# Seven block products in place of eight in the in-projections of two feed-forward stages

## The reference, cut to what matters

```python
def swiglu(x, w_in, w_out):                     # x (T, 1024), w_in (1024, 2*2816), w_out (2816, 1024)
    a, b = jnp.split(x @ w_in, 2, axis=-1)
    return (jax.nn.silu(a) * b) @ w_out

h = h + 0.5 * rms_norm_2(swiglu(rms_norm_2(h, g_ffn1_pre), w_ffn1_in, w_ffn1_out), g_ffn1_post)
...                                             # mixer
h = h + 0.5 * rms_norm_2(swiglu(rms_norm_2(h, g_ffn2_pre), w_ffn2_in, w_ffn2_out), g_ffn2_post)
```

## Time and profile before

| | us |
|---|---|
| three runs | 2240.53, 2245.5, 2245.35 |
| median | 2245.35 |
| the profiled execution, its own time | 2243.71 |
| its span in the trace | 2241.9 |
| PE busy in the span | 2103.8 (94%) |
| DVE busy | 993.0 (44%) |
| ACT busy | 725.9 (32%) |
| POOL busy | 624.9 (28%) |

### The profile page before, as it was taken

The page is one execution under the profiler, slowest core; times in us unless marked ns, Lnnn a source line. Parts: engine busy times, 40 slices in busy tenths (PEclk is TensorE's granted clock), DMA queues, the critical chain, the costliest instruction groups (busy, mean ns, idle before and its releaser), DMA issues.

```text
span 2241.9 us, 28339 instructions
## 1 busy us (share of the span) xinstructions
PE 2103.8 (94%) x11650; PEld 1754.6 (78%) x11650; DVE 993.0 (44%) x1483; ACT 725.9 (32%) x919; POOL 624.9 (28%) x152
## 2 busy tenths in 40 slices
PE   4999989999979999989999997999999979999997
PEld 3697777888757666589999996878788768888885
DVE  7374587656366666442222326232333252223224
ACT  6531345222245555332121123343232232221222
POOL 1331323344200000024433441221244314444440
PEclk6998999999979999989999997999999969999997
DMA  8122114554127999612222221211122212222220
GB/s 257 39 76 93 57 57 132 188 178 160 38 94 277 343 346 341 211 57 77 93 94 94 83 85 38 76 38 57 57 94 94 94 38 94 94 94 94 94 94 38
DMA packets 175177, 261.03 MB, mean 116 GB/s; under 512 B 12169, under 2 KB 140858, under 8 KB 175086
## 3 DMA queue, kind: packets, MB, share of 16 engines
q1 hardware_dynamic: 173550, 257.65, 34.5%
q10 hardware_dynamic: 1536, 2.10, 0.3%
HBM read 257.62 MB, written 2.11 MB: 116 GB/s over the span
## 4 chain that ended last, share of the span: by engine, by line
PE 89%; DVE 8%; ACT 2%; issue 1%; DMA 1%; DVEq 0%; SPq 0%; ACTq 0%
PE PS L704 68%; PE PS L1236 7%; PE PS L1258 4%; DVE Hf L2101 1%; PE PS L1390 1%; DVE macc L2167 1%; DVE Hf L2082 1%; PE PS L1202 1%; PE PS L764 1%; PE PS L1278 1%; DVE R L2113 1%; PE PS L1342 1%; PE PS L779 1%; PE PS L906 0%; PE PS L1160 0%
## 5 line engine op out<-in xcount | busy, mean ns | idle before, releaser
L663 POOL TENSOR_TENSOR w_lo<-w_raw,w_hi 128x2048 fp32r<-128x2048 f32 x133 | 620.3, 4664 | 1527.9 <-ACT w_hi L1509 1527.9
L704 PE MATMUL PS<-HH,w_hi 128*128 128x512 f32 (+1 forms) x1936 | 602.9, 349 | 31.8 <-DVE HL L2075 27.3
L704 PE MATMUL PS<-HL,w_hi 128*128 128x512 f32 (+1 forms) x1936 | 600.6, 348 | 0.0
L704 PE MATMUL PS<-HH,w_lo 128*128 128x512 f32 (+1 forms) x1936 | 597.6, 346 | 0.0
L1509 ACT ACTIVATE w_hi<-w_raw 128x2048 fp32r<-128x2048 f32 x133 | 254.8, 1915 | 713.5 <-DMA w_raw<-in_w_ffn_in 296.0
L704 PEld LDWEIGHTS PS<-HH,w_hi 128*128 128x128 f32 x1936 | 339.8, 191 | 84.4 <-issue 35.9
L704 PEld LDWEIGHTS PS<-HH,w_lo 128*128 128x128 f32 x1936 | 339.4, 191 | 45.8
L704 PEld LDWEIGHTS PS<-HL,w_hi 128*128 128x128 f32 x1936 | 339.3, 191 | 44.8
L2798 DVE TENSOR_TENSOR actf<-PS,sg 128x528 f32<-128x528 f32 (+1 forms) x44 | 30.8, 699 | 428.8 <-PE PS L704 428.8
L2809 DVE TENSOR_TENSOR yacc<-yacc,PS 128x528 f32<-128x528 f32 (+1 forms) x176 | 122.3, 695 | 106.2 <-PE PS L704 106.2
L2691 DVE TENSOR_TENSOR m_lo<-m_raw,m_hi 128x2048 fp32r<-128x2048 f32 x56 | 128.3, 2292 | 77.5 <-ACT m_hi L1842 76.8
(11 more groups left out here) (429 smaller groups left out, 2583.9 us busy)
## 6 DMA issues: line engine op xcount, KB each, us to landing
w_raw<-in_w_in SPq DMA_DIRECT2D x49, 1024.0 KB, 5.0
w_raw<-in_w_ffn_in SPq DMA_DIRECT2D x44, 1024.0 KB, 4.9
m_raw<-in_w_exp_gate SPq DMA_DIRECT2D x56, 512.0 KB, 4.2
m_raw<-in_w_exp_up SPq DMA_DIRECT2D x56, 512.0 KB, 5.3
m_raw<-in_w_exp_down SPq DMA_DIRECT2D x56, 512.0 KB, 4.8
w_raw<-in_w_ffn_out SPq DMA_DIRECT2D x22, 1024.0 KB, 4.8
mod_late<-in_w_mod SPq DMA_DIRECT2D x16, 1024.0 KB, 5.3
mod_early<-in_w_mod SPq DMA_DIRECT2D x8, 1024.0 KB, 11.8
```

The costliest lines, as they stand in the source:

```text
L663: pool.tensor_tensor(w_lo[:, s, :], w_raw[:, s, :], w_hi[:, s, :].bitcast(F32), ALU.subtract).then_inc(split, 1)
L704: ins = mm(o, l, r, **k)
```

## The change

The in-projection of a gate or up chunk is a product of a 2 by 2 block matrix of weights (two halves of the 1024 features by two halves of the 256 hidden ones) with a 2 by 2 block matrix of activations (the same two halves of the features by two halves of the tokens). Before, its eight block products are made one by one. After, there are seven (Strassen's method in the variant of Winograd): four sums of weight blocks, four of activation blocks, seven products, seven sums of products.

- Weights: DVE makes the four sums (`weight_sums`, each of 512 values a partition): one in place in `w_raw`, three in a new tile `wx_raw`. ACT and POOL split `wx_raw` as well (1536 values), after the chunk's 2048. ACT's high copy of `w_raw` and POOL's subtraction now wait for DVE's sums.
- Activations: `h_blocks` and `split_blocks` make and split the four sums once a stage, on DVE, ACT and POOL; each step handles four slices of T/2 columns, and PE waits for whole blocks.
- PE: 7 products of 12 matmuls of T/2 columns in place of 96 of 264 columns or 48 of 512. Two products share a PSUM slot; a chunk takes four slots, as many as there are.
- DVE: `block_sums` makes seven sums of 264 or 256 columns for each gate and up chunk, each with one operand in PSUM. ACT copies the first product to `fp` ahead of them. The silu is then computed by ACT in `sg` in place. DVE multiplies `actf` by `sg`, both now in SBUF and both tiles at once (1056 or 1024 values), ACT makes `ah`, DVE makes `al`.
- Order: DVE's `weight_sums` of the next gate chunk stands between the gate sums and the up sums of a unit, that of the next up chunk after the fourth down tile. Those of chunks 0 and 1 stand after tiles 4 and 6 of the step before the stage, that of chunk 2 before the clearing of `yacc`.

```diff
+            def h_blocks(n, T):
+                H, base = T // 2, HH_AT_FF[n]
+                pool.wait_ge(hh_ready, base + KT)
+                pool.tensor_tensor(HL[:, 4:8, 0:H], Hf[:, 4:8, 0:H], HH[:, 4:8, 0:H].bitcast(F32), ALU.subtract).then_inc(hp_ready, 1)
+                pool.tensor_tensor(HXr[:, 1, :, 0:H], Hf[:, 4:8, H:T], Hf[:, 0:4, H:T], ALU.subtract).then_inc(t3_ready, 1)
+                pool.wait_ge(hh_ready, base + KT + 3)
...
+            def split_seven(c, s, more=0):
+                pool.wait_ge(wx_ready, seven_made(c) + 1 + more * 2)
+                split_chunk(c, s, more)
+                pool.wait_ge(hix_done, seven_made(c) + 1 + more * 2)
+                pool.tensor_tensor(wx_lo[s][:, :, :, :], wx_raw[s][:, :, :, :], wx_hi[s][:, :, :, :].bitcast(F32),
+                                   ALU.subtract).then_inc(splitx, 1)
...
+            def seven_products(T, h_from=None):
...
+                for n in range(7):
+                    if n == 3:
+                        pe.wait_ge(splitx, xcount["n"] + 1 + xcount["more"])
...
+                    if n % 2 == 0:
+                        s = W.claim()
...
+                    for k in range(4):
+                        for x, (l, r) in enumerate(((0, 0), (0, 1), (1, 0))):
+                            ins = product(PS[:, s, n % 2, 0:H], left[l][n][:, k, :], right[r][n][:, k, :],
+                                          start=k == 0 and x == 0, stop=k == 3 and x == 2)
+                    if n % 2 == 1 or n == 6:
+                        W.made(ins)
...
             def next_hi():
...
+                if seven(c):
+                    act.wait_ge(wn_ready, seven_made(c) + 1 + rounds * 2)
+                else:
+                    act.wait_ge(w_in_sem[c % RING], 16 * (c // RING + 1) + rounds * 16)
...
+                if seven(c):
+                    act.wait_ge(wx_ready, seven_made(c) + 1 + rounds * 2)
+                    af(wx_hi[c % RING][:, :, :, :], wx_raw[c % RING][:, :, :, :], ACT.Copy).then_inc(hix_done, 1)
...
+                def unit(n, par):
+                    first_product()
                     next_hi()
+                    silu(n)
+                    first_product()
                     next_hi()
+                    product_hi(n, par)
...
+            def weight_sums(c):
...
+                dve.wait_ge(w_in_sem[s], 16 * (c // RING + 1) + more * 16)
+                a11, a12, a21, a22 = weight_blocks(w_raw[:, s, :])
+                x = wx_raw[s]
+                tt(x[:, 1], a11, a21, ALU.subtract)
+                tt(a21, a21, a22, ALU.add).then_inc(wn_ready, 1)
+                dve.wait_ge(wn_ready, n + more * 2)
+                L(tt(x[:, 0], a21, a11, ALU.subtract))
+                tt(x[:, 2], a12, x[:, 0], ALU.subtract).then_inc(wx_ready, 1)
...
                 W.release(stt(R[:, m, META:TALL], ps(s), modc[:, 40 + m:41 + m], R[:, m, META:TALL], ALU.mult, ALU.add))
+                if m in (4, 6):
+                    weight_sums(FF_AT[0] + m // 2 - 2)
...
+                def block_sums(dst):
+                    s0 = W.arrive()
...
+                    dve.wait_ge(fp_ready, n_["fp"] + n_["rounds"] * 2)
+                    tt(dst[:, 0, 0:H], fp[:, 0:H], PS[:, s0, 1, 0:H], ALU.add)
...
+                    s1 = W.arrive()
+                    u_ = L.mark(tt(fu[:, 0:H], fp[:, 0:H], PS[:, s1, 1, 0:H], ALU.add))
+                    L.wait(u_)
+                    w_ = L.mark(tt(dst[:, 0, H:T], fu[:, 0:H], PS[:, s1, 0, 0:H], ALU.add))
+                    dve.sem_inc(free[s0], 1)
...
+                def ups(n, par, more=0):
+                    block_sums(actf)
+                    dve.wait_ge(gate_silu, base + n + 1)
+                    tt(actf[:, :, 0:T], actf[:, :, 0:T], sg[:, :, 0:T], ALU.mult).then_inc(actf_ready, 1)
+                    dve.wait_ge(ah_ready, base + n + 1)
+                    tt(al[:, par, :, 0:T], actf[:, :, 0:T], ah[:, par, :, 0:T].bitcast(F32), ALU.subtract).then_inc(moe_act, 1)
...
+                def down(then=None):
                     for m in range(KT):
                         s = W.arrive()
                         y = sv(yacc[:, m, 0:T], T)
                         W.release(tt(y, y, ps(s, T), ALU.add))
+                        if m == 3 and then is not None:
+                            weight_sums(then)
...
+                def unit(n, c, par):
+                    gates()
+                    if c is not None:
+                        weight_sums(c)
+                    ups(n, par)
+                    down(None if c is None else c + 1)
```

More of the change, by code:

```diff
@@ L299, in build @@
         al = ar("al", 25344, [2, 2, TALL], F32R)
[L300 to L301 removed]
+        sg = hf("sg", 0, [2, TALL])
+        actf = hf("actf", 4224, [2, TALL])
+        fu = hf("fu", 8448, [TALL // 2])
+        fx = hf("fx", 9504, [TALL // 2])
+        fp = hf("fp", 10560, [TALL // 2])
+        HHx = ar("HHx", 33792, [3, 4, TALL // 2], F32R)
+        HLx = ar("HLx", 46464, [3, 4, TALL // 2], F32R)
+        HXr = ar("HXr", 46464, [3, 4, TALL // 2])
+        HLr = at("HLr", HL_AT, [KT, TALL])
+        wx_raw, wx_lo, wx_hi = [], [], []
+        for x, off in enumerate((77824, 90112, 65536)):
+            wx_raw.append(ar(f"wx_raw{x}", off, [3, 4, P]))
+            wx_lo.append(ar(f"wx_lo{x}", off, [3, 4, P], F32R))
+            wx_hi.append(ar(f"wx_hi{x}", off + 6144, [3, 4, P], F32R))
         TMH = ar("TMH", 0, [NTOK, KT, P], F32R)
@@ L472, in build, with seven, seven_made, weight_blocks @@
         block = ctx.enter_context(nc.Block())
+        FF_AT = (BEFORE_MOE, BEFORE_MOE + n_ff + n_p2 + n_m2 + n_wo)
+        HH_AT_FF = (2 * KT, 4 * KT + 12)
+        def seven(c):
+            for b in FF_AT:
+                if 0 <= c - b < n_ff - 1:
+                    return c - b < 2 or (c - b - 2) % 3 < 2
+            return False
+        def seven_made(c):
+            return sum(seven(x) for x in range(c))
+        def weight_blocks(w):
+            w = w.rearrange("p (k n) -> p k n", k=KT)
+            return w[:, 0:4, 0:P], w[:, 4:8, 0:P], w[:, 0:4, P:2 * P], w[:, 4:8, P:2 * P]
         def mod_dve(n):
@@ L1942, in swiglu @@
+                for n in range(2 * pairs + 1, units):
+                    unit(n, n % 2)
                     next_hi()
                     W.skip(KT)
-            norm(TALL, every)
+                next_hi()
+                W.skip(KT)
+                n_["ff"] += units
+            norm(TALL, every, split="blocks")
             swiglu(FF_UNITS, TALL)
@@ L2043, in _ @@
             norm(SEQ, y_real, split=False)
-            norm(SEQ, real, tiles=False)
-            swiglu(FF_UNITS, SEQ, last=True)
+            norm(SEQ, real, tiles=False, split="blocks")
+            swiglu(FF_UNITS, SEQ)
             norm(SEQ, y_real, split=False)
@@ L2114, in apply_rms @@
                     dve.wait_ge(r_ready, n_["r"])
+                elif split == "blocks":
+                    h_blocks(T)
                 elif split:
@@ L2839, in _ @@
             real = lambda k: R[:, k, META:TALL]
-            norm(TALL, every, c2(0))
-            swiglu(FF_UNITS, TALL)
+            norm(TALL, every, c2(0), split="blocks")
+            swiglu(0, FF_UNITS, TALL)
             norm(TALL, lambda k: yacc[:, k, 0:TALL], lambda k: gain1[:, k:k + 1], post=every)
@@ L2960, in _ @@
             norm(SEQ, lambda k: yacc[:, k, 0:SEQ], c2(3), post=real)
-            norm(SEQ, real, c2(4))
-            swiglu(FF_UNITS, SEQ)
+            norm(SEQ, real, c2(4), split="blocks")
+            swiglu(1, FF_UNITS, SEQ)
             norm(SEQ, lambda k: yacc[:, k, 0:SEQ], lambda k: gain2[:, k:k + 1], post=real)
```

237 lines of the change are left out of this document (165 added, 72 removed).

## The result

| | us |
|---|---|
| kernel before, median of 4 runs | 2245.43 (2240.53 to 2245.89) |
| changed kernel, median of 4 runs | 2335.64 (2334.07 to 2337.69) |
| ratio, 95% interval | 1.0407 (1.0389 to 1.0425) |
| span of the profiled execution | 2333.5, before 2241.9 |

The account below looks back on a forecast made before the run. Both feed-forward stages were taken as bound by PE's matmul count times spacing; -59.7 + 74 + 17 + 6 + 29 + 15 = +81.3 on 2243.71 gave 2325 us, own range 2290 to 2350, 8 in 10 range 2262 to 2368.

Parts of the forecast that it names:

- Part 1: Gate and up chunks of both stages: fewer or shorter PE matmuls save 32.3 and 27.4 us, together -59.7 us.
- Part 2: Units of both stages: DVE's product and subtraction to al wait for POOL's splits, PE pauses 3.8 and 4.3 us: +74 us.
- Part 3: Ahead of the stages: weight sums and POOL's splits delay the norm, PE starts 17 and 6 us later.
- Part 4: First chunk of each stage: PE waits for activation blocks, then for a slot; 14.3 us a stage, +29 us.
- Part 5: PE's clock: matmuls run at 1.2 GHz after the new pauses, +15 us, from bounds of 0 and 35.
- Rival 1: In the units DVE and POOL no longer meet: 2236 us, or 2201 if nothing meets ahead and in first chunks; chance 0.16.
- Rival 2: In the units one of the two waits goes, pause 1.6 us, no clock drops: 2268 us; chance 0.07.
- Rival 3: In the units POOL's extra split goes ahead of DVE's waiting product each time, all pauses slowed: 2362 us; chance 0.13.

Follow-up runs that it names:

- e1: Changed kernel with POOL subtracting only 8 values of each chunk and extra tile inside the stages, PE reading high parts for low (work left out): 2217.3 us, one run.
- e4: Changed kernel with POOL's subtraction inside the stages made in four instructions of 512 values per chunk and three per extra tile: 2254.7 us.
- e9: e6 with weight sums of chunks 0 and 1 earlier ahead of the first stage, and POOL's four activation-block instructions moved to DVE: 2209.2 us.
- e6: e3 with yacc cleared in the norm ahead of each stage instead of after the block sums of activations: 2224.3 us.
- e7: Changed kernel plus 12 useless matmuls after the fourth tile in each of the second stage's first ten down chunks: 2315.2 us.
- e3: Changed kernel with DVE's subtraction to al moved behind the fourth down tile's addition, and the next up chunk's weight sums behind the sixth: 2233.8 us.
- e10: e9 with four of eight yacc clearings before DVE's wait for the sum of squares, four after it, the gains' two products behind them: 2206.9 us.
- e2: Changed kernel with POOL subtracting only 8 of 1536 values of each extra tile, PE reading wx_hi for wx_lo (work left out): 2269.9 us, one run.

## Why the prediction was right, step by step

2325 was forecast and 2335.64 measured, inside the range and on the right side. The mechanism was right: DVE and POOL meet, and the addition that frees a PSUM slot stands behind it. That the sum came within 10 us is in part luck: the slow clock cost three times what was forecast, and the pauses less. Against the span of before the trace has +91.6 where the sum had +81.3. PE's rows at the start and end of the stages give the parts:

```profile
996.21 0.56 PE L780 MATMUL PS<-HH,w_hi 128*128 128x264 f32 x1 [6.84 <-DVE HL L2231]
...
1004.19 0.36 PE L780 MATMUL PS<-HH,w_hi 128*128 128x264 f32 x1 [2.87 <-DVE HL L2231]
...
1008.76 0.36 PE L780 MATMUL PS<-HHx,wx_hi 128*128 128x264 f32 x1 [2.88 <-DVE HLx L2231]
...
1020.17 0.56 PE L780 MATMUL PS<-HH,w_hi 128*128 128x264 f32 x1 [3.80 <-DVEq L2996]
...
1408.96 0.40 PE L780 MATMUL PS<-ah,w_lo 128*128 128x264 f32 x2
...
1888.01 0.55 PE L780 MATMUL PS<-HH,w_hi 128*128 128x256 f32 x1 [6.68 <-DVE HL L2231]
...
1911.35 0.55 PE L780 MATMUL PS<-HH,w_hi 128*128 128x256 f32 x1 [3.67 <-DVEq L2996]
...
2304.10 0.40 PE L780 MATMUL PS<-ah,w_lo 128*128 128x512 f32 x1
```

| part | forecast | measured | how |
|---|---|---|---|
| 1, matmuls | -59.7 | -61.0 | 50 spacings at 256 columns in 1943.74 - 1937.85: 117.8 ns |
| 2, pauses in the units | +74 | +68.7 | 9 x (3.33 + 0.2) and 9 x (3.90 + 0.2), means of the nine |
| 3, ahead of the stages | +17, +6 | +18.0, +3.5 | starts against before: 996.21 - 978.25; 1888.01 - 1408.96 against 1843.29 - 1367.73 |
| 4, first chunks | +29 | +27.1 | 23.96 less 10.26, and 23.34 less 9.90 |
| 5, clock outside the first chunks | +15 | +37.9 | what is left; the slow matmuls counted in the trace give 37 |
| PE's short waits of the first stage before, gone | none | -2.6 | 1367.73 - 978.25, less 3166 x 0.1222 |
| sum | +81.3 | +91.6 | |

**Part 1** held to 1.3 us; the matmuls did get fewer and no slower. The 109.2 ns at 256 columns, an estimate by the formula of the Trainium skill (TensorE: Matmul & The Clock Gate, Back-to-back issue gap), do not agree with the trace: 117.8 ns in this stream.

**Part 2** held link by link: both waits (3.59 and 3.28 less 1.26 us: 2.3 and 2.0, where 2.4 and 2.2 were forecast), the order in which DVE and POOL take turns, PE's pause at the fifth tile, nine a stage. The pauses are 3.5 and 4.1 us, where 3.8 and 4.3 were forecast; a unit takes 37.4 us, where 36.0 were forecast, the rest being slow clock. What the Trainium skill (SBUF — State Buffer, SBUF: two separate sides) says of a lock for a full instruction agrees with e1, e4 and e9: the product takes 1.24 us on average without POOL's splits, 1.49 beside short ones and 3.3 beside long ones.

**Part 3** held in size, less in its path. In the first stage chunk 1's sums met POOL twice, as forecast, but then it was not the additions of squares that were met. DVE's timeline:

```profile
962.62 4.51 DVE L2257 TENSOR_TENSOR wx_raw<-w_raw 128x512 f32<-128x512 f32 x1
967.04 3.90 DVE L2258 TENSOR_TENSOR w_raw<-w_raw 128x512 f32<-128x512 f32 x1
...
973.09 4.51 DVE L3061 TENSOR_SCALAR gain<-C 128x8 f32<-128x8 f32 x1
977.52 3.47 DVE L3062 TENSOR_SCALAR gain<-C 128x8 f32<-128x8 f32 x1
981.02 2.93 DVE L2268 TENSOR_TENSOR Hf<-Hf 128x528 f32<-128x528 f32 x4
```

Two products of 8 values (`gain`), which I had passed over, stood first in the queue and had to wait instead. The squares end at 983.95; 983.1 was forecast. In the second stage it was one addition of the norm ahead (four in 6.44 us).

**Part 4** held in its sum (13.7 and 13.4 us for 14.3 each), but by luck. The pauses are shorter than forecast, 2.87 and 2.88 us inside the first chunk of the first stage and 3.80 ahead of the second for the 5.1 forecast; with the smaller ones they make 10.7 and 9.3 us a stage. The other 3.0 and 4.2 us are matmuls at the slow clock, which part 4 had not in it and part 5 had in part. e6 and e9 confirm both causes of the pauses.

**Part 5** is the step that was mis-sized, 37.9 us for 15, and with the 7.2 us inside the first chunks some 45. Three things in it were too small. Each slow stretch was priced at the 1.7 us of the earlier trace rows; in the second stage they last 4.9 to 5.3 us, 2.3 to 2.5 us each. In the first stage, where it was taken only in part, seven of nine pauses are followed by one, of 3.3 us or more. And "PE is slowed while it waits for DVE anyway" holds for the first chunks only: behind a pause PE has its own path again, which e7 shows. Even the upper bound of 35 was too low.

**The rivals.** None of them happened in the changed kernel, but their prices can be compared. Rival 1 (2236, or 2201 if nothing meets) has the number that e3 reached by another way, 2233.8: there the two still meet, but off PE's path; e10 measured 2206.9. Rival 2 (2268) is e2, 2269.9: the pauses of its one wait were priced rightly, but that the sum is so near is partly luck. It had no clock in it, which cost 9 us in the units; against that PE's first stage starts 42.8 us after the first matmul of the last step before it, where the changed kernel needs 50.2, and the second stage 3.3 us earlier after the end of the first. Rival 3 did not occur: in all 20 units with an extra split waiting, DVE's product went ahead of it. Order decided, as said, and not the seven products: e3 has them all.

## What to carry to other kernels

Before you move work to an engine that looks idle, write one period of the schedule with start and end times, and mark each instruction of DVE that reads SBUF alone against each of POOL: a meeting costs the rest of the other's instruction. (What reads PSUM kept its time here, and so did the clearing of `yacc`, which reads nothing: 0.50 us an instruction from 1014.75 on, beside POOL's split from 1015.27 on, and the same in the kernel before.) What stands behind such an instruction in its queue pays for it, so put the additions that free PSUM ahead of what nobody needs yet, keep POOL's instructions short, or give a chain that the two would share to DVE alone. And price a pause of PE with the slow clock that follows it: here that was about half as much again as the pause, on average.

## What the runs showed that was not expected

- An operation's size is no protection: DVE's product of 8 values took 4.51 us behind POOL, and 0.15 us in e10 where it met nothing. The other way round POOL's 8 values in e2 took 1.22 us (0.21 alone) behind DVE's product.
- The pause that is followed by 1.2 GHz is not a matter of its length alone. In the changed kernel's first stage the two of 3.20 and 3.21 us had no such stretch, the seven from 3.25 us up had one; but in e7's first stage, which is the same code, one of 3.25 us had none, and in both traces it is the second and the ninth pause that go without. Before, one of 2.92 us had none. In e2's second stage, however, six of nine pauses of 1.8 to 2.7 us had one. None followed e2's nine pauses of 1.2 to 1.5 us in the first stage, nor e7's nine of 1.0 to 1.5 us in the second. What else enters was not tried.
- The slow stretch was longer in the second stage (4.9 to 5.3 us after pauses of 3.7 to 4.1) than in the first (3.3 to 3.8 us after 3.3 to 3.5, but once 5.9). Why is open.
